# Turning the gathered rows and hidden blocks of an expert layer by VectorE's 32 by 32 transposes instead of TensorE, in pairs 1 to 7

## The reference

```python
def expert_choice_ffn(h, w_router, w_gate, w_up, w_down):
    cap = EC_CAPACITY_FACTOR * T // N_EXPERTS
    aff = softmax(h @ w_router)
    gate_vals, idx = top_k(swapaxes(aff, 1, 2), cap)
    xs = h[bidx, idx]
    hid = silu(einsum('becd,edf->becf', xs, w_gate)) * einsum('becd,edf->becf', xs, w_up)
    out = einsum('becf,efd->becd', hid, w_down) * gate_vals[..., None]
    return zeros_like(h).at[bidx, idx].add(out)
```

## Time and profile before

| What | Value |
|---|---|
| Device time, median of 3 runs | 1004.88 us |
| Lowest and highest | 1000.21 and 1005.34 us |
| Span of the profiled execution, first to last instruction | 999.2 us |
| Median time less that span | 5.7 us |
| TensorE busy | 961.0 us, 96% of the span |
| VectorE, ScalarE, GpSimd busy | 362.7, 291.9 and 101.9 us |
| Granted TensorE clock, mean | 0.998 of full |
| Read from memory, written to it | 262.30 and 13.01 MB |

### The profile page before, as it was taken

One profiled execution on the slowest core, in us unless ns is written; L12 is line 12 of the kernel. 1 busy time (PEld: TensorE's weight loads), 2 busy tenths in 40 slices (PEclk: granted clock), 3 DMA queues, 4 the chain that ended last, 5 costly groups with the idle time before them and its releaser, 6 DMA issues.

```text
span 999.2 us, 18296 instructions
## 1 busy us (share of the span) xinstructions
PE 961.0 (96%) x7982; PEld 431.2 (43%) x7982; DVE 362.7 (36%) x825; ACT 291.9 (29%) x485; POOL 101.9 (10%) x112
## 2 busy tenths in 40 slices
PE   5999899999999899999899999999999999999996
PEld 4555556666666554463232322322323223232232
DVE  4477666463653663664021120210212102112115
ACT  5137756573653654323010100100101001010012
POOL 3200010000000011212002002011010110200200
PEclk9999999999999999999999999999999999999999
DMA  9990013504028541235999999999999999999982
GB/s 330 332 387 11 1 38 143 175 6 170 6 91 306 211 151 63 85 127 174 418 426 403 414 415 412 418 392 413 422 392 418 410 411 406 394 417 405 409 349 105
DMA packets 49395, 276.07 MB, mean 276 GB/s; under 512 B 4000, under 2 KB 12352, under 8 KB 37056
## 3 DMA queue, kind: packets, MB, share of 16 engines
q1 hardware_dynamic: 42000, 253.24, 63.0%
q0 software_dynamic: 5824, 16.81, 5.7%
q10 hardware_dynamic: 1520, 5.28, 1.4%
HBM read 262.30 MB, written 13.01 MB: 276 GB/s over the span
## 4 chain that ended last, share of the span: by engine, by line
PE 82%; DVE 7%; ACT 3%; DMA 3%; issue 2%; POOL 0%; SPq 0%; DVEq 0%; POOLq 0%
PE pa L568 54%; PE p L568 25%; DMA ring<-in_w_up_dram 2%; DMA ring<-in_w_ada_dram 1%; ACT reg_c L1199 1%; ACT reg_b L1199 1%; PE pa L1090 1%; ACT L1199 1%; PE p L1028 1%; DVE reg_c L1617 1%; DVE reg_c L1662 1%; ACT reg_d L1199 0%; DMA reg_c<-h_rows,row_s 0%; PE pa L1033 0%; PE p L712 0%
## 5 line engine op out<-in xcount | busy, mean ns | idle before, releaser
L568 PE MATMUL pa<-ring,reg_b 128*32 128x512 f32 (+1 forms) x3232 | 411.1, 593 | 1.3 <-ACT reg_b L1199 1.2
L568 PEld LDWEIGHTS pa<-ring,reg_b 128*32 128x32 f32 (+1 forms) x3232 | 129.2, 114 | 255.0 <-issue 254.5
L568 PE MATMUL pa<-reg_a,ring 128*128 128x512 f32 (+1 forms) x768 | 227.1, 450 | 5.9 <-DVE reg_a L1554 3.3
L568 PE MATMUL p<-ring,reg_b 128*16 128x512 f32 x1536 | 172.2, 592 | 2.6 <-DMA ring<-in_w_up_dram 2.5
L568 PEld LDWEIGHTS pa<-reg_a,ring 128*128 128x128 f32 x768 | 118.3, 191 | 98.2 <-issue 98.1
L1199 ACT ACTIVATE reg_b<-pa 128x512 f32<-128x512 f32 (+1 forms) x36 | 21.0, 608 | 423.3 <-PE pa L568 256.3
L568 PEld LDWEIGHTS p<-ring,reg_b 128*16 128x16 f32 x1536 | 45.1, 97 | 122.2 <-issue 121.2
L1956 DVE TENSOR_TENSOR reg_b<-reg_b,p 128x512 f32<-128x512 f32 x8 | 5.5, 689 | 235.1 <-PE p L568 235.1
L1199 ACT ACT_TABLE_LOAD x63 | 80.8, 1283 | 4.1 <-issue 2.8
L1980 DVE SCALAR_TENSOR_TENSOR reg_c<-pa,slot_s,reg_c 128x512 f32<-128x512 f32 x14 | 10.5, 751 | 101.5 <-PE pa L568 101.5
L1199 ACT ACTIVATE reg_c<-reg_c 128x320 f32<-128x320 f32 (+1 forms) x86 | 43.3, 574 | 10.1 <-DVE reg_c L1668 9.2
(11 more groups left out here) (304 smaller groups left out, 751.8 us busy)
## 6 DMA issues: line engine op xcount, KB each, us to landing
ring<-in_w_gate_dram SPq DMA_DIRECT2D x32, 2048.0 KB, 14.1
ring<-in_w_up_dram SPq DMA_DIRECT2D x32, 2048.0 KB, 12.2
ring<-in_w_down_dram SPq DMA_DIRECT2D x32, 2048.0 KB, 16.5
ring<-in_w_ada_dram SPq DMA_DIRECT2D x8, 2048.0 KB, 7.8
ring<-in_w_in_dram SPq DMA_DIRECT2D x6, 2048.0 KB, 19.9
ring<-in_w_ada_dram SPq DMA_DIRECT2D x8, 1024.0 KB, 12.9
ring<-in_w_out_dram SPq DMA_DIRECT2D x2, 2048.0 KB, 16.0
sum_rows<-reg_a ACTq DMA_DIRECT2D x5, 512.0 KB, 2.7
```

Of the source, the lines that this page charges most:

```text
L568: return nc.tensor.matmul(out, lhsT, rhs, start=start, stop=stop, **kw)
```

## The change

What is turned in pairs 0 to 7 of the hidden activations, and in pairs 1 to 7 of the gathered rows, is no longer turned by TensorE.

- `turn_group` (new, VectorE): four transposes. Each takes 32 partitions (q) of the source, from each of its 128-column tiles the 32 columns of block a, turns each 32x32 block and writes it to partitions 32a to 32a + 31, columns `to` to `to + 31` of each tile. Sixteen of them turn a 128x512 or a 128x1024 tile.
- `hidden` on VectorE: sample half 0, its transposes, sample half 1, its transposes, then the prompt rows and theirs. Its waits on silu_done and u_ps2 are now one for each half; the prompt rows wait for the last up slot to be freed.
- `next_rows` on VectorE: after `hidden`, 16 transposes of xg_s and 4 of xg_p into a new tile x_raw, once the gathers have landed. `next_rows` on ScalarE: eight sample and eight prompt scalings from x_raw.
- TensorE: `turn_hidden` and its calls go, `turn_rows` and `turn_prompt_rows` stay for pair 0's rows only. In the up sums of kh 1 the prompt part comes last. The down sums go to p67 instead of pa1, and their first waits are on ht2_done.
- GpSimd waits for xr_done instead of xs_ps and xp_ps before it gathers the rows of pairs 2 to 7.
- `add_rows` at the end uses pa1 and p67 in exchanged order.

```diff
+        x_raw = reg_d[:, 0:KT * (P + 32)].rearrange("p (k n) -> p k n", k=KT)
...
             for i in range(PAIRS - 1):
-                pool.wait_ge(xs_ps, i + 1)
+                if i == 0:
+                    pool.wait_ge(xs_ps, 1)
+                else:
+                    pool.wait_ge(xr_done, i)
                 gather_s(i + 1)
-                pool.wait_ge(xp_ps, i + 1)
+                if i == 0:
+                    pool.wait_ge(xp_ps, 1)
                 gather_p(i + 1)
...
-                dst = (pa[0], p67, pa[1], p45, pa[0])[i]
+                dst = (pa[0], pa[1], p67, p45, pa[0])[i]
...
                 use("u", 1)
-                prompt_sums("u", 1, rows_p, p45[:, 512:1024]).then_inc(u_ps2, 1)
                 sample_sums("u", 1, 0, xsT, pa[1]).then_inc(u_ps2, 1)
-                sample_sums("u", 1, 1, xsT, pa[1])
-                pe.wait_ge(hid_done, i * 3 + 2)
-                turn_hidden(pa[0], hid_s)
-                turn_hidden(pa[0][:, 512:1024], hid_p)
-                if not last:
-                    turn_rows(i + 1)
-                    pe.wait_ge(g_p, i * 16 + 32)
-                    pe.wait_ge(ht2_done, i * 3 + 1)
-                pe.wait_ge(hid_done, i * 3 + 3)
-                turn_hidden(p45, hid_s[:, 512:1024])
-                if not last:
-                    turn_prompt_rows(pa[0])
+                sample_sums("u", 1, 1, xsT, pa[1]).then_inc(u_ps2, 1)
+                prompt_sums("u", 1, rows_p, p45[:, 512:1024])
                 use("d", 0)
-                pe.wait_ge(ht2_done, i * 3 + 2)
-                sample_sums("d", 0, 0, hsT, pa[1])
-                sample_sums("d", 0, 1, hsT, pa[1])
+                pe.wait_ge(ht2_done, i * 3 + 1)
+                sample_sums("d", 0, 0, hsT, p67)
+                sample_sums("d", 0, 1, hsT, p67)
                 pe.wait_ge(ht2_done, i * 3 + 3)
                 if not last:
                     prompt_sums("d", 0, hidden_p, p45[:, 512:1024])
...
+            def next_rows(i):
+                act.wait_ge(xr_done, i)
+                for k in range(KT):
+                    r = A(xsT[:, k, :], x_raw[:, k, 0:P], ACT.Identity, bias=x_mod[:, 1, 0, k:k + 1], scale=x_mod[:, 0, 0, k:k + 1])
+                r.then_inc(xs_done, 2)
+                for k in range(KT):
+                    r = A(xpT[:, k, :, :].rearrange("p e n -> p (e n)"), x_raw[:, k, P:P + 32], ACT.Identity,
+                          bias=x_mod[:, 1, 1, k:k + 1], scale=x_mod[:, 0, 1, k:k + 1])
+                r.then_inc(xp_done, 1)
...
+            def turn_group(dst, src, q, to):
+                rows, at = slice(32 * q, 32 * q + 32), src.rearrange("p (k n) -> p k n", n=P)
+                for a in range(4):
+                    blk = slice(32 * a, 32 * a + 32)
+                    r = V.transpose(dst[blk, :, to:to + 32], at[rows, :, blk])
+                return r
+            def next_rows(i):
+                dve.wait_ge(g_s, i * 16 + 16)
+                for q in range(4):
+                    turn_group(x_raw, xg_s, q, 32 * q)
+                dve.wait_ge(g_p, i * 16 + 16)
+                turn_group(x_raw, xg_p, 0, P).then_inc(xr_done, 1)
             def hidden(i):
...
                 for half in range(2):
+                    dve.wait_ge(silu_done, i * 3 + half + 1)
+                    dve.wait_ge(u_ps2, i * 2 + half + 1)
                     hv, cols_ = hid_s[:, half * 512:half * 512 + 512], slice(half * 512, half * 512 + 512)
                     V.tensor_tensor(in_fours(hv), in_fours(hv), fours(pa[1][:, cols_]), ALU.mult).then_inc(hid_done, 1)
+                    dve.wait_ge(hid_done, i * 3 + half + 1)
+                    for q in range(4):
+                        r = turn_group(hsT[:, 4 * half:4 * half + 4, :], hv, q, 32 * q)
+                    r.then_inc(ht2_done, 1)
+                dve.wait_ge(silu_done, i * 3 + 3)
+                s, turn = chunk("u", 1, 1)
+                dve.wait_ge(freed[s], i * 2 + turn + 1)
+                V.tensor_tensor(in_fours(hid_p), in_fours(hid_p), fours(p45[:, 512:1024]), ALU.mult).then_inc(hid_done, 1)
+                dve.wait_ge(hid_done, i * 3 + 3)
+                for q in range(4):
+                    r = turn_group(hpT, hid_p, q, 32 * q)
+                r.then_inc(ht2_done, 1)
```

More of the change, by code:

```diff
@@ L343, in program @@
         silu_done, hid_done = sem("silu_done"), sem("hidden_done")
-        ht2_ps, ht2_done = sem("hidden_turned"), sem("hiddenT_ready")
+        ht2_done, xr_done = sem("hiddenT_ready"), sem("next_rows_turned")
         out_done, out_free = sem("out_rows_done"), sem("out_rows_free")
@@ L1029, in turn_rows, with turn_prompt_rows @@
                 r.then_inc(xs_ps, 1)
-            def turn_prompt_rows(dst):
+            def turn_prompt_rows():
                 for k in range(KT):
-                    r = nc.tensor.transpose(dst[:, k * 32:(k + 1) * 32], xg_p[:, k * P:(k + 1) * P], ident[0:32, 0:32])
+                    r = nc.tensor.transpose(p67[:, k * 32:(k + 1) * 32], xg_p[:, k * P:(k + 1) * P], ident[0:32, 0:32])
                 r.then_inc(xp_ps, 1)
             def add_rows(i):
-                dst = (pa[0], p67, pa[1], p45, pa[0])[i]
+                dst = (pa[0], pa[1], p67, p45, pa[0])[i]
                 if i == NT - 1:
@@ L1076, in prompt_sums @@
                             r = mm(dst[32 * q:32 * q + CP, :], xT(k, e), w, k == 0, k == KT - 1)
-                            if k4 == 3 and half == 1 and (m, kh) != ("u", 1):
+                            if k4 == 3 and half == 1:
                                 r.then_inc(freed[s], 1)
@@ L1086, in hidden_p @@
                     return hpT[:, k % 4, at:at + CP]
[L1088 to L1091, removed]
                 if head:
@@ L1110, in pair @@
                     pe.wait_ge(g_p, 16)
-                    turn_prompt_rows(p67)
+                    turn_prompt_rows()
                     sample_sums("g", 1, 1, xsT, pa[0], (2, 3)).then_inc(g_ps, 1)
@@ L1158, in pair @@
                     use("d", 1)
-                    sample_sums("d", 1, 0, hsT, pa[1]).then_inc(d_ps, 1)
-                    sample_sums("d", 1, 1, hsT, pa[1]).then_inc(d_ps, 1)
+                    sample_sums("d", 1, 0, hsT, p67).then_inc(d_ps, 1)
+                    sample_sums("d", 1, 1, hsT, p67).then_inc(d_ps, 1)
                     prompt_sums("d", 1, hidden_p, p45[:, 512:1024])
@@ L1968, in _ @@
             V.memset(p45[:, 512:1024], 0.0)
-            prompt_rows_in(0, p67)
+            prompt_rows_in()
             with dve.Fori(0, PAIRS - 1) as i:
                 hidden(i)
-                rows_in(i + 1)
-                prompt_rows_in(i + 1, pa[0])
+                next_rows(i + 1)
                 dve.wait_ge(out_free, i + 1)
@@ L2021, in add_rows @@
             def add_rows(i):
-                src = (pa[0], p67, pa[1], p45, pa[0])[i]
+                src = (pa[0], pa[1], p67, p45, pa[0])[i]
                 if i == 0:
```

46 lines of the change are left out of this document (15 added, 31 removed).

## The result

| | before | with the change |
|---|---|---|
| median of four executions, us | 1003.75 (1000.21 to 1005.34) | 1028.76 (1022.84 to 1031.71) |
| span of the profiled execution | 999.2 | 1028.8 (its time: 1030.52) |
| ratio with its 95% interval | | 1.0251 (1.0225 to 1.0278) |
| one pair, down sums to down sums | 64.88 | 68.3 |

The change makes the kernel slower by 25 us, 2.5%. The forecast was 12 us slower, with a range that holds the result. One execution of one experiment, `a2_half_fill`, took 1265 us at a mean clock of 0.752, and the ratio of that experiment is taken without it.

What follows compares the result with a forecast made beforehand. TensorE's matmul stream was taken to bound the kernel, loads just keeping up. Stall +1.0 and rows +0.4 us in seven pairs (+9.8), plus 2.1 in the last, gave +12 on 1004.9: 1017 us, range 1001 to 1048.

Steps and rivals of the forecast that it cites:

- The place of the loss: TensorE before the down sums' first prompt part: a new stall of 4.0 us in place of 2.95 of turning.
- the third group: VectorE's last 16 hidden-block transposes, those of the prompt rows, forecast to end 17.7 us after the first up half.
- T: Moment when the first sample half of the up sums is ready; the down sums could start at T + 6.86.
- The price of a transpose: On VectorE: 0.32 us with 128 elements a partition and 0.45 with 256, each counted in full without overlap.
- The doubled element: VectorE's transposes cost twice per element, 0.40 and 0.67 us, giving 1078 us; chance 0.07.
- the first rival: VectorE's transposes overlap or take below 0.30 us, stall under 2.95 us, loads then bound at 1002 us; chance 0.23.
- The wait for the rows: At the next pair's start, gate sums wait for ScalarE's scaled rows: 0.4 us in each of pairs 0 to 6.
- full clock as the likeliest case: TensorE's sums stay at full clock, with transposes from 0.30 to 0.38 us; chance 0.58.
- its upper end: Top of the forecast range, 1048 us: a transpose of 0.37 us with some of the clock's price.
- the clock's rival: TensorE's clock falls in the new stalls, sums run 3.3 us at half speed, +9 us more, 1026; chance 0.12.
- The bound of 2.8 us: Whole kernel: the last load lands at 965.8, so the change can gain 2.8 us at most unless loads get faster.
- The base: Starting time of 1004.9 us: the profiled span of 999.2 plus 5.7 to the median, taken as unchanged.

Runs made afterwards that it cites:

- a2_half_fill: Changed kernel with 16 useless matmuls on TensorE before the wait for the third group of transposes; 1022.13 us, ratio 1.0189.
- a1_fill: Changed kernel with 32 useless matmuls on TensorE before the wait for the third group of transposes; 1018.09 us, ratio 1.0156.
- a4_rows_only: Kernel before, with only the next pair's rows turned by VectorE and scaled by ScalarE, hidden blocks still on TensorE; 995.44 us, ratio 0.9923.
- a3_quarter_turns: Changed kernel with only a quarter of the transposes of hidden activations and next rows; 994.72 us, ratio 0.9911.
- b2_early_rows: Changed kernel with rows gathered and turned earlier, scaled after the up sums, and hidden groups ordered half 0, prompt, half 1; 1002.76 us, ratio 0.9994.
- b1_hidden_only: Changed kernel with hidden blocks still turned by VectorE, but next rows turned by TensorE, in the stall; 1018.38 us, ratio 1.0155.
- c2_rows_early_only: Changed kernel with only the next rows gathered, turned and scaled early, group order kept; 1017.12 us, ratio 1.0159.

## Why the prediction was right or wrong

**The place of the loss was right.** It named a stall of TensorE before the prompt part of the down sums, ended by the third group, 4.0 us in place of 2.95 of turning; it is 3.78. The third group ends at T + 17.4, forecast T + 17.7.

**The price of a transpose was right**, in part by luck, since it was the middle between the times of two other instructions: 0.32 and 0.45 us, against 0.316 and 0.449. No transpose overlaps the next: a single one is 303 ns long and the next starts after 316. The doubled element (0.40 and 0.67) is ruled out by the same rows, the overlap of the first rival too. VectorE is busy 20.1 us more in the stretch of 65 us, forecast 21. Twenty transposes of the rows end at T + 26.5, forecast T + 26.7.

**The wait for the rows** was forecast at 0.4 us a pair and does not occur in the changed kernel, because TensorE comes 2.6 us later than planned. At full clock it is 0.93 (`a1_fill`). The step mis-sized there is ScalarE's: sixteen scalings take 5.62 us, not 5.0. The eight sample ones (481 ns each) start 0.385 apart and the eight prompt ones (399 ns) 0.305, where I had 0.346 and 0.265. The saving by fewer elements was right, 0.08 us; what I took from the rows of scalings out of PSUM was 0.04 too low for both.

**The step that failed: full clock as the likeliest case.** From one idle stretch of 2.5 us with the clock at 1.00 and a fall 3.3 us after the last matmul, I gave the clock's fall a chance of 0.12. But the stretch foreseen, 4.0 us, was longer than both; by my own rows the fall was the likely case and not the rival. The size failed as well. I took 3.3 us at half speed, a loss of 1.65 and 1.3 net, to reach 1026. The clock was at half for 6.82 us, 5.33 of them with sums, a loss of 2.62, and nothing came back at the rows, as that wait was not there to be hidden under. With the measured terms the sum for the profiled execution is 7.7 for the stalls and 20.5 for the clock; without the clock it would have been 7.7 + 0.93 x 7 = 14, and `a1_fill`, at full clock, shows 15 over the kernel before. So the mechanism of the forecast was worth 14 to 15 us where it said 12, and the other 10 or 11 are the clock's. That the range holds 1028.8 is owed to its upper end, which stood for a transpose of 0.37 us and not for what happened; the clock's rival named the right cause and came within 3 us, at a chance of 0.12.

**The bound of 2.8 us was wrong**, though it did not enter the forecast. It took a DMA share of 1.01 for a fixed rate and so 965.8 for a fixed landing. Waits of SyncE's queue before the change, 500 to 945 us (us in total, times, longest):

```profile
SPq L426 <- PE p L568: 338.1, 34, 12.4
SPq L426 <- PE pa L568: 66.3, 7, 11.8
```

In that stretch the queue stands 41 times until TensorE frees a slot, and TensorE stands for no load at all. The loads went at TensorE's pace, 410 GB/s, and the share of 1.01 did not tell it. Two kernels landed the last load sooner, `a4_rows_only` by 3.3 us and `a3_quarter_turns` by 3.0 (962.8), at 414 GB/s instead of 410, and their times fell by 8 and 9. The way in which the loads bind held (in `a3_quarter_turns` and `b2_early_rows` TensorE waits for them, and no pair goes faster than 63.8 us), but at 1 us a pair below where I had it. So the first rival's 1002 was too high: with a quarter of the transposes the change stands at 994.7.

**The base** was slightly off. The 5.7 us between the median and the profiled span are not a fixed part: an execution's time is its span and 1.7 us, once 2.7 (1030.52 and 1028.8), and the rest is the spread between executions.

What stays open: why the DMA engines show the same share of busy time at 410 and at 414 GB/s; and what, besides the length of an idle stretch, decides whether the clock falls. That the length alone does not decide is shown by `a2_half_fill`, `b1_hidden_only` and `c2_rows_early_only`, where equal stalls of one run end both ways. Whether it is the moment of the stall was not tried.

## What to carry to other kernels

Price a new stall of TensorE twice, once as time in which it stands and once as the slower work behind it: here 0.8 us more of standing brought 2.6 us of slow matmuls in every pair. When work is moved to an engine that has time, move the part whose result is needed late (the next pair's rows, 8 us gained) and not the part that stands between two uses of the full engine (the hidden blocks, 15 us lost), or reorder until each piece is asked for only after the queue has come to it. A DMA share of 1.0 says that the loads are busy and not that they can go no faster. Look whether TensorE ever waits for a load; if it never does, only a run with TensorE sped up shows where they bind.

## What was unexpected of the hardware

- The clock fell with idle stretches of 2.03 to 2.11 us (`a2_half_fill`, three of eight) and 2.11 to 2.13 us (`b1_hidden_only`, four of seven), and after 2.69 us in pair 0 of the change, but not after 2.50 there before, nor after 2.86 there in `a1_fill`. The Trainium skill's page TensorE: Matmul & The Clock Gate tells in its section Why this matters for your kernels to leave no idle gaps between bursts of matmuls. The runs agree, and the shortest gap with a fall behind it, 2.04 us, is shorter than those that the page warns of.
- A fall lasted 3.4 us (`a2_half_fill`, `b1_hidden_only`, `c2_rows_early_only`) or 6.8 (the change). The first costs 1.7 us of matmul time, the second 2.5 to 2.7, since 1.5 us of it pass while TensorE still stands.
- A stall of one length made the clock fall in every pair (3.78 us, the change) or in every second (3.75 to 3.83, `c2_rows_early_only` from 650 us on). The same program differed by 10 us between executions with its mean clock, 0.986 at 1020.1 and 0.968 at 1030.0.
- ScalarE's scalings from SBUF to SBUF start 0.385 us apart with 128 columns and still 0.305 apart with 32: a quarter of the elements for four fifths of the time.
